# Encoder block on one core: the first output weights' split placed later in two engine orders, and the state-space kernel matrix loaded in four parts

## The reference

```
x = x + 1/2 * SwiGLU_1(RMSNorm(x))
h = RMSNorm(x); [q | k | v | u] = h @ w_in
attn = sliding-window attention over 128 frames, with sinks and ALiBi
ssm: 32 groups x 16 channels, complex diagonal state of 64 per group
     s_t = lam_bar * s_(t-1) + b_bar u_t ;  y = Re(C s) + D u
     z = gelu(y) ;  out = z * sigmoid(z @ w_glu + b_glu)
x = x + concat(RMSNorm(attn), RMSNorm(ssm)) @ w_out
x = x + 1/2 * SwiGLU_2(RMSNorm(x)) ; final RMSNorm
```

## Time and profile before

| | |
|---|---|
| runs of the kernel before | 1688.15 us median of 3 (1685.57 to 1692.62) |
| the profiled execution | 1684.99 us, of which the span from first to last instruction is 1683.3 us |
| PE busy | 1616.9 us, 96% of the span |
| DVE, ACT, POOL busy | 1102.6, 719.7, 530.0 us |
| mean granted PE clock | 0.976 of full |

### The profile page before, as it was taken

One profiled execution on the slowest core, in us unless ns is written; L12 is line 12 of the kernel. 1 busy time (PEld: TensorE's weight loads), 2 busy tenths in 40 slices (PEclk: granted clock), 3 DMA queues, 4 the chain that ended last, 5 costly groups with the idle time before them and its releaser, 6 DMA issues.

```text
span 1683.3 us, 21959 instructions
## 1 busy us (share of the span) xinstructions
PE 1616.9 (96%) x7540; PEld 1326.9 (79%) x7540; DVE 1102.6 (66%) x1711; ACT 719.7 (43%) x1317; POOL 530.0 (31%) x953
## 2 busy tenths in 40 slices
PE   7999999999999999999767999999999999999998
PEld 5778888888888887887556788788888888888887
DVE  5866667767678878325664547765666556677765
ACT  6544344343444445346415434534343434344452
POOL 4004788877767875100232332000000000000011
PEclk8999999999999999999868999999999999999999
DMA  6345334333696544712655035123222332785443
GB/s 211 122 100 104 113 129 163 119 113 119 218 348 201 138 109 113 263 51 83 113 86 177 13 100 187 64 94 132 101 100 101 127 123 94 265 298 161 121 110 122
DMA packets 158152, 231.63 MB, mean 138 GB/s; under 512 B 18401, under 2 KB 96865, under 8 KB 154465
## 3 DMA queue, kind: packets, MB, share of 16 engines
q1 hardware_dynamic: 154976, 222.66, 41.5%
q0 software_dynamic: 3072, 7.62, 2.4%
HBM read 156.09 MB, written 74.15 MB: 137 GB/s over the span
## 4 chain that ended last, share of the span: by engine, by line
PE 85%; DVE 6%; DMA 2%; ACT 2%; issue 2%; SPq 2%; POOL 1%; POOLq 0%; DVEq 0%; ACTq 0%
PE bank L1141 27%; PE bank L1143 27%; PE bank L1142 27%; DVE hblo L2237 1%; DVE ws_lo L2201 1%; DMA raw<-in_w_out_dram 1%; DVE htmp L2148 1%; PE bank L1446 1%; SPq L1096 1%; PE bank L1468 1%; PE bank L1599 0%; PE bank L1163 0%; ACT hT_hi L1661 0%; DMA x_in<-in_x_dram 0%; PE bank L1398 0%
## 5 line engine op out<-in xcount | busy, mean ns | idle before, releaser
L1141 PE MATMUL bank<-hbhi,ws_lo 128*128 128x512 f32 x1056 | 414.1, 392 | 9.2 <-DVE ws_lo L2201 4.9
L1142 PE MATMUL bank<-hblo,ws_hi 128*128 128x512 f32 x1056 | 411.8, 390 | 0.0
L1143 PE MATMUL bank<-hbhi,ws_hi 128*128 128x512 f32 x1056 | 411.7, 390 | 0.0
L2794 POOL TENSOR_TENSOR ssq<-ssq,sqt 128x512 f32<-128x512 f32 x25 | 38.0, 1521 | 669.8 <-ACT sqt L1645 668.5
L1141 PEld LDWEIGHTS bank<-hbhi,ws_lo 128*128 128x128 f32 x1056 | 198.7, 188 | 56.2 <-issue 7.0
L1141 PE MATMUL bank<-d_hi,ws_lo 128*128 128x512 f32 x616 | 240.7, 391 | 0.0
L1143 PE MATMUL bank<-d_hi,ws_hi 128*128 128x512 f32 x616 | 239.8, 389 | 0.0
L1142 PE MATMUL bank<-d_lo,ws_hi 128*128 128x512 f32 x616 | 239.6, 389 | 0.0
L1143 PEld LDWEIGHTS bank<-hbhi,ws_hi 128*128 128x128 f32 x1056 | 198.7, 188 | 41.7
L1142 PEld LDWEIGHTS bank<-hblo,ws_hi 128*128 128x128 f32 x1056 | 198.8, 188 | 41.2 <-issue 0.5
L1713 ACT ACTIVATE loc<-bank 128x512 f32<-128x512 f32 x160 | 95.6, 598 | 254.9 <-PE bank L1143 254.9
(11 more groups left out here) (296 smaller groups left out, 2613.9 us busy)
## 6 DMA issues: line engine op xcount, KB each, us to landing
b_scratch<-loc SPq DMA_DIRECT2D x42, 1024.0 KB, 7.3
d_in<-b_scratch SPq DMA_DIRECT2D x154, 256.0 KB, 3.1
raw2a<-in_ff_w_up_dram SPq DMA_DIRECT2D x44, 512.0 KB, 4.7
loc<-in_ff_w_gate_dram SPq DMA_DIRECT2D x36, 512.0 KB, 4.5
x_scratch<-xT SPq DMA_DIRECT2D x6, 2048.0 KB, 11.1
dw_lo_place<-in_ff_w_down_dram SPq DMA_DIRECT2D x8, 1024.0 KB, 7.5
xT<-x_scratch SPq DMA_DIRECT2D x8, 1024.0 KB, 6.8
x_in<-in_x_dram SPq DMA_DIRECT2D x8, 512.0 KB, 6.8
```

The costliest lines, as they stand in the source:

```text
L1141: nc.tensor.matmul(o, wl, rh, start=first, stop=False, skip_group_check=chain)
L1142: nc.tensor.matmul(o, wh, rl, start=False, stop=False, skip_group_check=chain)
L1143: return nc.tensor.matmul(o, wh, rh, start=False, stop=last, skip_group_check=chain)
L2794: pool.tensor_tensor(ssq_of(norm, h), ssq_of(norm, h), sqt_of(norm, a), ALU.add).then_inc(ssq_done, 1)
```

## The change

Two strings change: on ACT, `W2` moves from ahead of `y0` to behind `g0`; on DVE, from between recurrences 1 and 2 to behind `z1`. On SPq, `load_u8(3)` moves ahead of the store of `kst`. `Mt` is loaded in four parts of eight groups, eight DMAs of 64 KB each, on two semaphores in turn; the third part is issued only when the first has landed, the fourth only when the second has. `Y` of batch b waits for its own part alone.

```diff
-MIXER_ACT = steps("k0 k1 k2 k3 O6 k4 k5 k6 k7 C7 O7 W1 s0 s1 s2 s3 s4 s5 s6 s7 W2 y0 y1 g0 y2 g1 y3 g2 g3")
-MIXER_DVE = steps("d0 d1 d2 d3 d4 d5 d6 d7 R0 W1 R1 W2 R2 R3 b3 a0 a1 z0 z1 z2 z3")
+MIXER_ACT = steps("k0 k1 k2 k3 O6 k4 k5 k6 k7 C7 O7 W1 s0 s1 s2 s3 s4 s5 s6 s7 y0 y1 g0 W2 y2 g1 y3 g2 g3")
+MIXER_DVE = steps("d0 d1 d2 d3 d4 d5 d6 d7 R0 W1 R1 R2 R3 b3 a0 a1 z0 z1 W2 z2 z3")
@@
-    m_loaded = sem("m_loaded")
+    m_loaded = [sem(f"m_loaded{i}") for i in range(2)]
@@
+        load_u8(3)
+        k_v = k_d.rearrange("g h c -> h g c")
         sp.wait_ge(k_taken, 8)
         sp.wait_ge(zero_stored, 48)
-        sp.dma_start(k_d.rearrange("g h c -> h g c")[:, :, (T - 1) * GH:], kst[:, :, :]).then_inc(k_stored, 16)
-        load_u8(3)
+        sp.dma_start(k_v[:, :, (T - 1) * GH:], kst[:, :, :]).then_inc(k_stored, 16)
         sp.wait_ge(k_stored, 16)
-        for t in range(T):
-            c0 = (T - 1 - t) * GH
-            sp.dma_start(Mt[t * GH:(t + 1) * GH, :, :],
-                         k_d.rearrange("g h c -> h g c")[:, :, c0:c0 + P]).then_inc(m_loaded, 16)
+
+        for b in range(4):
+            if b >= 2:
+                sp.wait_ge(m_loaded[b % 2], 16 * T)
+            for t in range(T):
+                c0 = (T - 1 - t) * GH
+                sp.dma_start(Mt[t * GH:(t + 1) * GH, 8 * b:8 * b + 8, :],
+                             k_v[:, 8 * b:8 * b + 8, c0:c0 + P]).then_inc(m_loaded[b % 2], 16)
@@
-            pe.wait_ge(m_loaded, 16 * T)
+            pe.wait_ge(m_loaded[b % 2], 16 * T * (b // 2 + 1))
```

## The result

| | before | after |
|---|---|---|
| first series of runs, us | 1688.15 median of 5 (1685.57 to 1692.86) | 1678.68 median of 5 (1672.01 to 1679.29) |
| ratio after to before | | 0.9923 (95%: 0.9899 to 0.9948) |
| profiled execution, its span, us | 1684.99, 1683.3 | 1678.77, 1677.1 |
| mean granted PE clock, profiled execution | 0.976 | 0.974 |

By the ratio the change is worth 0.8% (0.5 to 1.0), about 13 us. The ratios here are estimated over all executions and are not the quotient of the two medians, which lie 9.5 us apart. The forecast was 1674.5 us, with 1668 to 1683 as its range: the median of 1678.68 is inside it, 4.2 us above the forecast.

What follows compares the result with a forecast made beforehand. PE bounds the kernel, its longest wait 21.6 us for recurrence 2: 14.0 us sooner, less 4.2 beside POOL, plus 2.9 no longer held by `Y0`, less 0.1, gives 12.6; forecast 1674.5 us, range 1668 to 1683.

Steps and rivals of the forecast that it cites:

- `W2` held recurrence 2, and with it PE: On DVE, recurrence 2 waits for the split of an early `w_out` unit; moving it starts the recurrence 14.0 us sooner.
- Recurrences beside POOL take 10.6 us: On DVE, recurrences 2 and 3 beside POOL's rotations were charged 10.6 us each; recurrence 2 took 6.4 with POOL idle.
- Starts of `Y0` and `Y1`, 842.5 and 853.1: On PE, each output round starts behind its recurrence; `Y1` at 853.1 is 12.7 us ahead of its old start.
- `Mt` hidden: SyncE's queue: at 112 GB/s the four parts land near 832, 837, 841 and 846, so `Y0` doesn't wait.
- The rival by which each pays its landing in turn: Loads of `Mt`: each of 32 DMAs lands before the next moves, 67 us; kernel about 10 us slower, 1698; chance 5%.
- What the parts are worth: Loading `Mt` in four parts: about 1.6 us by itself; beside the order edit, a single `Mt` makes `Y1` 2.5 us later.
- `W2` in its new place costs 0 to 0.3 us: On ACT behind `g0`, the moved copy delays `y2` by 1.1 us at most, nearly all hidden; 0.1 us was taken.
- The chain of 25.1 us behind `Y1`: From the end of `Y1` through `y1`, `g1`, `y3`, `g3` to PE's last first-GLU part: 25.1 us, links unchanged.
- the likely case: PE's clock low in `Y0` and `Y1`, at its upper level in `Y2` and `Y3`: gain of 10 to 15 us, 68%.
- a clock that comes up later: PE's clock low to the end of `Y3`: `Y2`, `Y3` 9.2 us each, gain 6.5, 1680.5 us; 12% for gains of 4 to 9.
- 5.1 us each for `Y2` and `Y3`: On PE, the last two output rounds run at the upper clock, 2.4 GHz, 5.1 us each, ending at 872.3.
- The other clock rival: PE's clock up from the start: `Y1` takes 5.1 instead of 8.8 us, 3.7 more gain, 1671 us; chance 10%.

Runs made afterwards that it cites:

- e1: Kernel before with only the two order strings changed, `Mt` still one load of eight DMAs: 1676.47 us median against 1690.05, ratio 0.9936.
- e2: Changed kernel with both order strings put back, so `Mt` is loaded in parts but `W2` stays in its old place: 1685.99 us, ratio 0.9959 to the kernel before.
- e3: The changed kernel run again, nothing edited: 1676.02 us median against 1690.05 for the kernel before, ratio 0.9914.
- e6: Changed kernel with `Mt` in eight DMAs of 256 KB, every `Y` waiting for all of it: 1680.73 us, ratio 0.9945 to the kernel before.
- e4: Changed kernel plus extra matmuls in PE's three pauses (23 between halves of `I3`, 34 before `Y0`, 22 before `Y1`): 1670.26 us, ratio 0.9887 to the kernel before.
- e7: Changed kernel with four semaphores and without SyncE's two waits between the parts of `Mt`: 1676.09 us, ratio 0.9928 to the kernel before.
- e5: Changed kernel plus extra matmuls in the pauses ahead of `Y0` (23 and 34), none between `Y0` and `Y1`: 1674.78 us, ratio 0.9928 to the kernel before.

## Why the prediction was right, point by point

**`W2` held recurrence 2, and with it PE: shown.** e1 takes it away alone: DVE's idle time is gone, `Y1` begins 8.1 us sooner and the time falls by 0.6% (0.4 to 0.9).

**Recurrences beside POOL take 10.6 us: shown.** 10.5 and 10.6 us in the changed kernel; 6.4 us for recurrence 2 in e2, where POOL is idle. The extra is 4.1 us where 4.2 were charged: 1.1 in the second addition (1.75 us instead of 0.68) and about 1.0 in each of the three scans behind it.

**Starts of `Y0` and `Y1`, 842.5 and 853.1: 842.04 and 852.54.** In that execution the work ahead lies about 0.4 us earlier; in e3's it is 842.66 and 853.17.

**`Mt` hidden: right, with a wrong rate.** I took the rate of the large DMAs, 112 GB/s, for the small ones too. They issue one in 0.5 us and land in 2.6, and the last was issued at about 840; PE never waited. By these figures the first part was down at about 831, as forecast (832), and the last near 842.5, not 846. The rival by which each pays its landing in turn (67 us) is refuted by 32 DMAs in 18 us.

**What the parts are worth: wrong.** By themselves I put 1.6 us, for the earlier start. e2 shows 5.1 us at recurrence 2, since the `w_out` unit behind them in the queue lands sooner too. Beside the first edit I put `Y1` 2.5 us later with a single `Mt`; e6 shows 3.8, and e1, where the load also starts later, 5.2. In the sum of the change neither counted.

**`W2` in its new place costs 0 to 0.3 us: nothing in the rows speaks against it.** In e4, the tightest case, ACT has copied it by 863.72 and then still waits 0.24 us for `Y2`; DVE has idle time behind its part (874.99, then nothing until 883.01 in the changed kernel). No run takes it out.

**The chain of 25.1 us behind `Y1`: shown** in e3: 861.94 to 887.20 is 25.3 us, with the 0.1 for `y2` in it. In e4 it was 25.7.

**The clock: the mechanism was named, its share was mis-sized.** I forecast 1674.5 us with `Y2` and `Y3` at the upper clock as the likely case (68%) and gave 12% to a clock that comes up later, at 1680.5 for all of it. The profiled execution and three others, 1678.1 to 1679.3 us with clocks of 0.974 and 0.975, are that case (the three by their time and mean clock), and only one of five, 1672.01 us with 0.979, is like the forecast. The price of the rival was right: 6.5 us of gain forecast, 6.2 measured in the profiled execution. The term that failed is "5.1 us each for `Y2` and `Y3`", taken from one execution of before: of the 19 of e1's series about four in five had a lower mean clock than it. The pause between `Y0` and `Y1`, which I named as the reason, isn't needed for it, and doesn't force it. e1, e2 and e6 have no such pause (14.06, 16.62 and 12.94 us of waiting, then the four rounds without a break), and in their profiled executions the clock was low to the end of `Y3`; e3 and e7 have the pause of 1.24 us, and the clock came up in them at 861.9 and at about 872. That the range held is partly luck: it was drawn to take in both clock cases, but the weights of 68 and 12 were the wrong way round for this series, and the median came out near because both kernels have both cases. The other clock rival, up from the start, was priced at 3.7 us more; e4, which brings that about by extra work, has its last GLU part 887.20 - 883.85 = 3.4 us ahead of e3's.

**The same mistake hides in the base.** I added the gain to a mean of 1684.99 and 1688.15. The later series give the kernel before 1690.05, 1689.38 and 1691.9 us as median, and the changed kernel 1676.02: a difference of 14.0 us in the series that has both, 9.5 in the first series, 12.6 forecast.

What stays open: what decides in an execution when the clock comes up in the thin work of `Y`. The same instructions had it at 861.9 (e3) and, in the changed kernel's first profile, only at about 888, well after `Y3` had ended at 880; e7's, with the same work on PE, had it at about 872, in `Y3`. Of the seven profiled executions without extra matmuls, three (before, e3, e7) had the clock up by the end of `Y3` and four (the changed kernel's first, e1, e2, e6) did not. The waits ahead of `Y0` were 21.6, 7.5 and 7.5 us in the three, 7.5, 14.1, 16.6 and 12.9 us in the four: their length doesn't sort them. Denser work ahead of the rounds does move it, as e4 shows.

## What to carry to other kernels

An instruction that waits for a transfer nobody needs yet blocks all that is queued behind it on its engine: look at what the first idle row of an engine waits for, and ask whether the rows behind it need that. When a stall is removed, price the work that moves forward beside its new neighbours, not its old ones (here 6.4 us became 10.5), and walk down to the next two things that are late. And where PE's clock is low in part of a profile, take several executions before a duration at either level goes into a sum.

## What the runs showed of the hardware

- The granted clock differs between executions of one program: in the changed kernel it was up from 861.9 to beyond the end of `Y3` in e3 and low there until about 888 in its first profile, and each output round took 5.1 or 9.2 us accordingly. Unbroken work was not enough to bring it up: in e1 PE was busy from 848.5 to beyond 892 at 1.2 GHz. It also rose with PE idle: in the changed kernel's first profile PE did nothing from 888 to 892, and the clock was up for most of that and low again for the GLU part at 893.4.
- Denser matmuls (128x512, 22 to 34 of them) in the pauses kept the clock at the upper level through all four rounds in the profiled execution of e4, whose six times lie within 2.4 us; after a pause of 5.3 us it was low again in e5's. Extra work on PE made the program 5.8 us faster by the medians of e3 and e4.
- 2.1 MB in rows of 512 bytes, from DRAM into 16 partitions at a time, moved faster in 32 DMAs of 64 KB (18 us from first issue to last landing, 2.6 us from issue to landing) than in 8 of 256 KB (23 us, 13.1 us). In the two stretches shown, all transfers together made 124 GB/s with an engines' share of 0.52, and 100 GB/s with 1.20. The Trainium skill (SBUF, "The DMA setup-cost knee") asks for 128 partitions and the largest single transfer; here, with 16 partitions, the trace goes the other way on size, and that the share per byte was more than twice as high with the large ones is seen but not explained.
- In a recurrence beside POOL, DVE's second addition, with two SBUF inputs, took 1.75 us instead of 0.68, and the three scans behind it 1.4 to 1.5 instead of 0.4; the multiplications with one input from PSUM kept their 0.66 to 0.68. POOL pays too: its multiplication at 841.30 took 1.72 us instead of 1.26. This agrees with the Trainium skill (SBUF, "Who interferes with whom").
